# The shared expert's gate and up matmuls moved into the LN1 stage, a ring of eight weight matrices, and a routing mask by replacement

## What is computed

```python
mix = concat([y_pool, y_conv, y_mem]) @ w_out
x1 = layer_norm(alpha * x + mix, ln1_g, ln1_b)            # LN1
scores = sigmoid(x1 @ w_router)                            # 64 experts
_, idx = top_k(scores + router_bias, 8)
sel = take_along_axis(scores, idx)
gates = sel / sum(sel) * 2.5
# every expert e, for its tokens: 1024 -> 256 -> 1024
y_e = (silu(x1 @ w_gate[e]) * (x1 @ w_up[e])) @ w_down[e] * gate
shared = (silu(x1 @ w_gate_sh) * (x1 @ w_up_sh)) @ w_down_sh   # every token
x = layer_norm(alpha * x1 + routed + shared, ln2_g, ln2_b)     # LN2
```

## Time and profile before

| | us |
|---|---|
| median of 3 runs | 1502.26 (1501.83 to 1504.17) |
| profiled execution | 1498.6 |
| its span, first to last instruction | 1497.0 |
| PE busy in it | 1355.4 (91%) |
| DVE busy | 989.9 (66%) |
| ACT busy | 776.2 (52%) |
| POOL busy | 469.7 (31%) |
| mean granted TensorE clock | 0.942 of 2.4 GHz |

### The profile page before, as it was taken

The page is one execution under the profiler, slowest core; times in us unless marked ns, Lnnn a source line. Parts: engine busy times, 40 slices in busy tenths (PEclk is TensorE's granted clock), DMA queues, the critical chain, the costliest instruction groups (busy, mean ns, idle before and its releaser), DMA issues. The chain is left out here.

```text
span 1497.0 us, 25821 instructions
## 1 busy us (share of the span) xinstructions
PE 1355.4 (91%) x6447; PEld 1115.0 (74%) x6448; DVE 989.9 (66%) x1164; ACT 776.2 (52%) x1031; POOL 469.7 (31%) x433
## 2 busy tenths in 40 slices
PE   8968937799879999999999999999999999999965
PEld 7856626577767887888888788888888887788842
DVE  4599656367776377676577645557577577677718
ACT  4122155221133376776577646657677577677710
POOL 0000010136644224333343333333333434433321
PEclk9988967798879999999999999999999999999978
DMA  6121050222345489898889978888899899998745
GB/s 228 43 70 56 0 187 8 85 85 85 86 157 200 148 295 342 260 337 283 250 300 318 344 229 250 255 250 249 267 305 323 280 323 349 327 322 272 233 150 211
DMA packets 77249, 327.89 MB, mean 219 GB/s; under 512 B 22720, under 2 KB 22832, under 8 KB 51744
## 3 DMA queue, kind: packets, MB, share of 16 engines
q1 hardware_dynamic: 41360, 251.05, 44.9%
q0 software_dynamic: 34704, 72.23, 20.0%
q10 hardware_dynamic: 1152, 4.19, 0.7%
HBM read 294.65 MB, written 67.34 MB: 242 GB/s over the span
## 5 line engine op out<-in xcount | busy, mean ns | idle before, releaser
L1494 PE MATMUL ps<-wgu,xTe 128*128 (+1 forms) x2496 | 597.7, 395 | 14.1 <-ACT wgu L696 9.7
L1494 PEld LDWEIGHTS ps<-wgu,xTe 128*128 128x128 f32 x2496 | 463.5, 189 | 111.2 <-issue 18.5
L1512 PE MATMUL ps<-wdn,hT 128*128 (+1 forms) x1236 | 297.3, 389 | 0.0
L1197 DVE TENSOR_TENSOR wgu<-raw,wgu (+1 forms) x130 | 292.1, 2289 | 5.5 <-issue 3.1
L1512 PEld LDWEIGHTS ps<-wdn,hT 128*128 128x128 f32 x1236 | 232.0, 188 | 48.2
L696 ACT CAST wgu<-raw (+1 forms) x130 | 250.0, 1925 | 29.1 <-SPq L395 28.4
L1202 DVE TENSOR_TENSOR xTe<-ps,xTe 128x512 fp32r<-128x512 f32 x210 | 134.9, 684 | 140.6 <-ACT xTe L748 138.0
L1197 DVE TENSOR_TENSOR wdn<-raw,wdn (+1 forms) x65 | 149.0, 2293 | 53.6 <-ACT wdn L741 52.5
L753 ACT ACTIVATE ysb<-ps,idx 128x512 f32<-128x512 f32 x188 | 119.1, 685 | 118.7 <-PE ps L1512 118.7
L539 POOL DMA_INDIRECT xa_d<-ysb,idx x48 | 88.0, 1834 | 259.6 <-ACT ysb L753 208.6
L539 POOL DMA_INDIRECT xb_d<-ysb,idx x47 | 88.5, 1883 | 241.7 <-ACT ysb L753 224.7
(11 more groups left out here) (200 smaller groups left out, 1148.2 us busy)
## 6 DMA issues: line engine op xcount, KB each, us to landing
raw<-in_w_gate SPq DMA_DIRECT2D x64, 1024.0 KB
raw<-in_w_up SPq DMA_DIRECT2D x64, 1024.0 KB
raw<-in_w_down SPq DMA_DIRECT2D x64, 1024.0 KB
wraw<-in_w_in SPq DMA_DIRECT2D x10, 512.0 KB, 3.3
xin<-in_x SPq DMA_DIRECT2D x8, 512.0 KB, 7.0
wraw<-in_w_kv SPq DMA_DIRECT2D x8, 512.0 KB, 3.3
raw<-in_w_out SPq DMA_DIRECT2D x4, 1024.0 KB, 7.9
xres<-in_x SPq DMA_DIRECT2D x8, 512.0 KB
```

The costliest lines, as they stand in the source:

```text
L1197: V.tensor_tensor(dst, raw_, hi.bitcast(F), ALU.subtract).then_inc(done, 1)
L1494: last = mm(ps[:, 2 + s, :], xTe[:, s, st, d], wgu[:, w, mo, d].rearrange("p a n -> p (a n)"), start=(d == 0 and st == 0 and mo == 0), sto ...
L1512: last = mm(ps[:, 5 + h, :], hT[:, s, st, c], wdn[:, w, mo, c, h * 512:(h + 1) * 512].rearrange("p a n -> p (a n)"), start=(c == 0 and st ...
```

## The change

**PE's order in the LN1 stage.** A round now does both halves of the projection of tile t + 1, then the transposes of tile t, the rank sums of tile t-1, the gate and up matmuls of the shared expert for tile t-1 from its `x1T` (now two buffers), and the logits of tile t. The weights stand in `wsh`, the results in banks 1 and 4; ACT's silu and DVE's product `hxs` follow in the LN1 loops. The rows are not loaded and transposed a second time.

**The rest of the shared expert.** Seven tiles' hidden transposes and down matmuls follow the stage; the eighth tile's lie in the first routed step. ACT itself issues the stores of their results.

**Normalisation.** ACT's part goes; DVE subtracts the mean and multiplies by the gain, then multiplies by the reciprocal root and adds the offset.

**Routing.** The eight best scores are replaced by a large negative number, and the mask is where the array changed. Addresses come from the largest eight of mask x (list start + rank).

**Ring.** `raw` is a ring of eight matrices; matrix n of expert e has place (3e + n + 1) mod 8. SP requests the loads one matrix at a time, in the order in which the places come free. The loads of LN2's gain and offset are issued after the last split of weights, before it was after the item tables.

```diff
--- before.py
+++ after.py
-        xTe = at("xTe", 96, [128, 2, 2, ND, 128], R)
-        raw = at("raw", 112, [128, 2, 3, 2048])
+        xTe = at("xTe", 184, [128, 2, 2, ND, 128], R)
+        raw = at("raw", 96, [128, SLOTS, 2048])
...
-        x1T = at("x1T", 152, [128, 2, ND, 128], R)
+        wsh = at("wsh", 96, [128, 2, ND, 512], R)
+        wshr = at("wshr", 112, [128, ND, 512])
+        wdnr = at("wdnr", 72, [128, 2, D])
+        x1T = at("x1T", 144, [128, 2, 2, ND, 128], R)
+        hxs = at("hxs", 184, [128, NT - 1, XD])
...
+        def shared_bank(u):
+            return (1, 4)[u % 2] if u < NT - 1 else 3
+        def slot_of(e, n):
+            return (3 * e + n + 1) % SLOTS
...
-            for n, w in enumerate(("sh_gate", "sh_up", "sh_down")):
-                sp.dma_start(raw[:, 0, n], a[w]).then_inc(s_rwd[0] if n == 2 else s_rw[0], 16)
+            for n, w in enumerate(("sh_gate", "sh_up")):
+                sp.dma_start(wshr[:, :, n * XD:(n + 1) * XD],
+                             a[w].rearrange("p (c n) -> p c n", c=ND)).then_inc(s_shw, 16)
...
-            def load_expert(e, s, nth):
...
-                sp.wait_ge(s_glo, 2 * e - 2)
-                load("w_gate", 0, s_rw[s])
-                load("w_up", 1, s_rw[s])
-                sp.wait_ge(s_rw[1 - s], 32 * nth)
-                sp.sem_inc(s_ready, 1)
-                sp.wait_ge(s_dlo, e - 1)
-                load("w_down", 2, s_rwd[s])
-                sp.wait_ge(s_rwd[1 - s], 16 * nth)
-                sp.sem_inc(s_dready, 1)
+            def load_expert(e0, rounds):
+                e = e0 + SLOTS * rounds
+                if e0 == 2:
+                    sp.wait_ge(s_lg, NT)
+                    sp.wait_ge(s_gu, NT)
+                elif e0 >= 4:
+                    sp.wait_ge(s_glo, 2 * e - 4)
+                load(e, 0, slot_of(e0, 0))
+                for n in range(2):
+                    landed(e0 - 1, n, rounds)
+                sp.sem_inc(s_ready, 1)
+                if e0 >= 4:
+                    sp.wait_ge(s_dlo, e - 2)
+                load(e, 1, slot_of(e0, 1))
+                landed(e0 - 1, 2, rounds)
+                sp.sem_inc(s_dready, 1)
+                if e0 >= 3:
+                    sp.wait_ge(s_glo, 2 * e - 3)
+                load(e, 2, slot_of(e0, 2))
...
@@ scalar @@
+            def shared_silu(u):
+                act.wait_ge(s_gu, u + 1)
+                if 2 <= u < NT - 1:
+                    act.wait_ge(s_h, u - 1)
+                dst = hss[:, u % 2] if u < NT - 1 else hs[:, 1]
+                nc.scalar.activation(dst, ps[:, shared_bank(u), 0:XD], ACT.Silu).then_inc(s_silu, 1)
...
-                    nc.scalar.activation(xres[:, t % 2], xres[:, t % 2], ACT.Identity,
-                                         bias=rs[:, 1:2], scale=rs[:, 0:1]).then_inc(s_hat, 1)
...
+            for t in range(NT):
+                if t + 2 < NT:
+                    mix_hi(t + 2)
+                if t == NT - 1:
+                    shared_silu(t - 1)
+                x1_hi(t)
+                if 1 <= t < NT - 1:
+                    shared_silu(t - 1)
+                scores_of(t)
...
+            for u in range(NT - 2):
+                hidden_hi(u + 1)
+                if u == 2:
+                    act.wait_ge(s_ready, 2)
+                    gate_up_hi(1, 0)
+                    gate_up_hi(1, 1)
+                if u >= 2:
+                    act.wait_ge(s_ysh[u % 2], 16 * (u // 2))
+                act.wait_ge(s_dn, u + 1)
+                y_out(u % 2, 1.0 / ALPHA)
+                put_shared(u)
...
@@ vector, route @@
-                step(V.max_index(idxu[:], top8[:], sb_[:]))
-                settle()
-                step(V.tensor_copy(idxf[:, u], idxu[:]))
-                settle()
-                step(V.tensor_tensor(oh[:], iotaE[:].unsqueeze(1).to_broadcast([128, K, E]),
-                                     idxf[:, u].unsqueeze(2).to_broadcast([128, K, E]), ALU.is_equal))
-                settle()
-                step(V.tensor_reduce(maskf[:], oh[:].rearrange("p k e -> p e k"), AX.X, ALU.add))
-                settle()
-                step(V.tensor_copy(maskb[:], maskf[:]))
+                step(V.match_replace(rest[:], top8[:], sb_[:], -1e30))
+                settle()
+                step(V.tensor_tensor(maskb[:], rest[:], sb_[:], ALU.not_equal))
+                step(V.tensor_tensor(maskf[:], rest[:], sb_[:], ALU.not_equal))
...
@@ vector, LN1 loop @@
-                step(V.tensor_tensor(xres[:, r], xres[:, r], g1[:], ALU.mult))
-                settle()
-                V.tensor_tensor(xres[:, r], xres[:, r], b1[:], ALU.add).then_inc(s_x1, 1)
+                if t >= 1:
+                    x1_lo(t - 1)
+                step(V.scalar_tensor_tensor(x, x, mv[:, 0, 0:1], g1[:], ALU.subtract, ALU.mult))
+                v.wait_ge(s_pw, 2 + t)
+                settle()
+                V.scalar_tensor_tensor(x, x, rs[:, 0:1], b1[:], ALU.mult, ALU.add).then_inc(s_x1, 1)
+                if t >= 2:
+                    rank(t - 2)
+                    shared_hidden(t - 2)
+                if t >= 1:
+                    route(t - 1)
...
+            rank(NT - 1)
+            hidden_lo(0)
+            item_tables()
+            hidden_lo(1)
+            hidden_lo(2)
+            item_tables_out()
+            hidden_lo(3)
+            gate_up_lo(1, 0)
+            hidden_lo(4)
+            gate_up_lo(1, 1)
+            hidden_lo(5)
+            hidden_lo(6)
...
@@ tensor @@
+            for t in range(NT):
+                if t + 1 < NT:
+                    for h in range(2):
+                        project(t + 1, h)
+                else:
+                    shared_gate_up(t - 1)
+                x1_transposed(t)
+                if t >= 1:
+                    ranks(t - 1)
+                if 1 <= t < NT - 1:
+                    shared_gate_up(t - 1)
+                logits(t)
+            shared_gate_up(NT - 1)
...
+            for u in range(NT - 1):
+                if u + 1 < NT - 1:
+                    hidden_transposed(u + 1)
+                down(u, u % 2, 0)
+                if u == 1:
+                    item_tables()
```

More of the change, by code:

```diff
@@ L48 @@
 RING = 8
+SLOTS = 8
 ALWAYS = (NT + E) // RING
@@ new lines, in _ @@
+            pe.wait_ge(s_oe, 2 * HEADS)
+            for h in range(2):
+                project(0, h)
+            pe.wait_ge(s_wrl, 1)
+            for t in range(NT):
+                if t + 1 < NT:
+                    for h in range(2):
+                        project(t + 1, h)
[7 more added lines that the diff above has]
+                logits(t)
```

502 lines of the change are left out of this document (239 added, 263 removed).

## The result

The changed kernel takes **1479.95 us** (median of 4 runs, 1477.48 to 1480.28) against 1502.05 for the kernel before in the same session: ratio 0.9849, 95% interval 0.9824 to 0.9875. It is 22 us faster; the forecast was 44. The profiled execution took 1479.69 us, its span is 1478.1 us.

What follows compares the result with a forecast made beforehand. PE bounds it: the LN1 stage in small pieces at clock 0.85, the routed loop with 24.3 us of stalls. 1498.6 - 25.5 (earlier routed start) - 19 (ring) = 1454.1 profiled, 1458 us for the median; range 1444 to 1486.

Steps and rivals of the forecast that it cites:

- two cases in the 1470s: Rivals: DMA engines limit the routed loop, 1474 us, chance 0.14; the new LN1 stage throttles, 1473 us, chance 0.12.
- two bounds of the stage: Gain at the first routed start: 30 us with no half clock and first down 2 us late; 8 at worst.
- signs named: Next profile: routed start 492 to 500 us, rounds 20 to 21, downs some 4 apart, weight waits under 8.
- The LN1 rounds: Six equal PE rounds in the LN1 stage, together 20.2 us each, 121.3 in all, without the former 2.39 us waits.
- I charge it once: Half clock after PE waits in the LN1 stage or the downs: 4.9 us, added once, moving the start to 496.5.
- The row of downs: Seven shared downs after the LN1 stage: 19.1 us of matmuls plus exposed latencies, 35.2 us, ending at 487.3.
- the last scatters, the tables and the first gather: Beside the row of downs: estimated done some 8 us before the downs end, counted as nothing.
- gathers come late behind weights: Rival: loop gathers delayed by one more weight matrix in flight, 2.0 us late on half the items, 1554 us; chance 0.06.
- The ring: Eight matrices in the routed loop: two more lie ready per run of single-item experts, absorbing 19 of 24.3 us of stalls.
- Routing by replacement: DVE in the LN1 rounds: some 1.5 us a tile less, hidden under PE, taken at nothing.
- The new stage throttles: Rival: PE's waits at tile 0, tile 7 and in the downs each bring half clock, 1473 us; chance 0.12.
- The engines limit the loop: Rival: full DMA engines, not the ring, limit the routed loop; gain 3 instead of 19 us, 1474 us; chance 0.14.

Runs made afterwards that it cites:

- e5: Changed kernel with tile 7's transposes ahead of tile 6's shared gate and up, and hidden low halves ahead of last rank and item tables: 1472.14 us.
- e8: e1 plus only e5's new order of the last round; the last rank stays ahead of the first hidden half: 1461.17 us.
- e1: Changed kernel with SP's loads of expert 2 held until the stores of the first four shared tiles have landed: 1464.4 us.
- e2: Changed kernel with four buffers of their own for shared results 2 to 5, so ScalarE waits for no store: 1477.55 us.
- e3: Changed kernel, eight ring places kept, but SP waits before loads as in the kernel before, never more than six matrices ahead: 1494.2 us.
- e6: Changed kernel with e1's hold of the weights and both of e5's new orders together: 1464.5 us.
- e7: e6 with own buffers for shared results 2 to 5 and the weights held until GpSimd's first gather is issued: 1464.26 us.
- e9: e6 with a scatter address buffer for each tile instead of two in turn: 1464.12 us.
- e10: e7 with a scatter address buffer for each tile: 1460.35 us.
- e11: e8 with a scatter address buffer for each tile: 1462.31 us.
- e12: e10 with the weights of expert 2 held until the first gathered rows have landed, not until their gather is issued: 1455.51 us.
- e4: Changed kernel with two unused one-hot operations and a reduction added back to each tile's routing on DVE: 1478.05 us.

## Why the prediction was right and where it failed

**Direction and range: right, the range in part by luck.** The shared matmuls and the ring both gain, and 1479.95 lies in 1444 to 1486. Its upper part was there for two cases in the 1470s; the half clock was one of them, the wait for the store, 8.3 us, was in none. The likeliest time, 1458, was 22 us too low. For the profiled execution the sum was 1454.1 and the time is 1479.69: 25.6 us to account for. They are 21.3 in the start of the first routed gate and up (496.5 forecast, 517.8 measured), 2.4 in the loop (2.3 of them the half clock in the first routed gate and up), 1.9 in the tail. Of the signs named, the rounds and ACT's waits for weights (3.4 us) came as forecast, the start and the distance of the downs did not. The two bounds of the stage were added up wrongly: from the terms named they are 33 and 7, not 30 and 8, and the measured 4.2 lies below either.

**The LN1 rounds: right.** Six rounds were put at 20.2 us each. Five take 20.1 without a gap; the first takes 22.8, because its projection still runs at half clock for a part (13.89 us instead of 11.16). What fell is "I charge it once". Half clock came at the logits of tile 0 and at those of tile 7 (rows of the profile after), about 5 us each: the last shared gate and up end at 460.4, 8.3 us past the 452.1 in which neither was charged. 4.9 of these 8.3 had been charged. e5 and e8 took the second away: the order alone gives 6.2 us ahead of the downs. The Trainium skill, "TensorE: Matmul & The Clock Gate", section on HAM oscillation, has waits between bursts paid again by the clock; the traces agree for these two places.

**The row of downs: the step that failed.** It was put at 35.2 us with 4.3 behind it, and took 57.4 (460.44 to 517.83), 17.9 more. The largest part is at the fourth down. I had put 3.7 us there, for two conversions on ACT; they took 3.7 (479.79 to 483.49), and then ACT waited 8.4 more for a landed store, so that the fourth down started 12.0 us after PE was ready: 8.3 over. Then 4.0 are half clock in two downs (4.51 and 5.46 us instead of 2.97 and 3.01), 3.1 the first down (7.8 us after the last gate and up instead of 4.7, of which 2.7 are the late silu; in e1, e2 and e3 it is 5.1), 2.1 the opening of the first routed item (6.4 us instead of 4.3), and 0.4 the rest. The working looked at latencies of engines alone, and had a row that said otherwise: in the earlier trace rows a load of 0.5 MB behind three weight matrices was waited for until 12.2 us after its issue. I used it for the gathers of the loop and not for the stores. It asked of no queue what its transfers wait for, though two of them lie on the path: the stores of `ysb`, which has two buffers and now takes a result every 4 us instead of every 9.3, and "the last scatters, the tables and the first gather run beside the downs; I estimate them done some 8 us before the downs end, and count nothing". The gather was issued at 499.35 us, 12.2 us before the downs ended (511.6), and did not hold PE there. Where the store no longer does, this chain can set the start: in e2, e6, e7, e9, e10, e11 and e12 PE waits for gathered rows (in e1, e3 and e8 it does not). The hold alone (e1) makes the row 43.9 us, 4.4 over the forecast. e12 starts 2.7 us ahead of my 496.5, but with the new order of the last round in it.

**The cause is what SP does, shown by e1, and by e3 with fewer weights.** I counted SP's weight requests in the loop and not at the place where the change releases them. Before, SP requested expert 2 from 446.98 to 450.37 us, and then no weights until

```profile
489.29 0.33 SPq L390 DMA_DIRECT2D raw<-in_w_gate  x1
```

Now the request of expert 2 waits for the last shared gate and up (`s_gu` in the diff; the ring lies over `wsh`), so it goes out just ahead of the downs, and there is room for four matrices at once. The rival "gathers come late behind weights" was this mechanism; I placed it in the loop, where no row of after shows it, and gave it 0.06. Beside it I cited the Trainium skill, "DMA: Bandwidth & Descriptors", section on queues and rings: an engine takes turns between queue rows by packet. Here that did not protect a small transfer: 18.0 us for 0.5 MB behind weights, 2.7 (e1) to 4.9 (e6) at most without them. The measurement decides; which part of the way is slow there (169 GB/s at a share of 1.04) stays open.

**The ring: right.** 19 was forecast, 16.6 came in the loop; e3 shows that it is the ring.

**Routing by replacement: right**, priced at nothing (e4).

**The other rivals.** "The new stage throttles" gave 1473 for three more half clocks, 14.7 us. Half clock came at all three places it names, 4.9, 5.0 and 4.0 us, of which 4.9 had been charged: this rival, with a chance of 0.12, holds 9.0 of the 21.3 us at the start, and the wait for the store 8.3. That the two are separate causes e1 shows, which takes the store's wait and leaves the half clock at tile 7 (logits 5.15 us). "The engines limit the loop" is refuted by 3.4 us of waits at the same share of 0.87.

## What to carry to other kernels

When work is taken out from between short steps, ask each queue what it will start at the moment when the cover goes: a prefetch that is released at the head of a row of small stores, scatters and gathers delays them all, and one wait on SP was worth 10 to 15 us (e1), against 22 for the whole change. Follow the chain to its last transfer: a hold that ends one transfer too early gave e6, e7 and e9 nothing on e1 for the waits they removed, and moved to the landing of that transfer it gave 4.8 us (e12 against e10, medians of two sessions). A buffer only moves such a wait on to the next chain; price both chains before choosing between more buffers and a later prefetch. A wait of PE that one group of matmuls can cover may be worth more than its length: 1.94 us at tile 7 were worth 6.2 in e5, because the groups behind it then also ran at full clock.

## What the runs showed of the hardware

In the changed kernel a wait of 2.38 us and one of 1.94 us between dense matmuls were each followed by half clock for about 10 us of matmuls, a loss of 5 us; in e2 the same 1.94 us cost 3.4. A wait of 2.1 to 2.2 us between two downs was followed by half clock in e7 and e9 (4.6 us instead of 3.0) and not in e6 and e8, so the length of the wait alone does not tell. DMA engines at a busy share of 1.04 moved 169 GB/s in one stretch and 376 at 1.02 in another: the share tells that engines are occupied, not that they move much. A scatter of 128 pairs keeps GpSimd for 1.28 us, and GpSimd waited 5.3 us (e10) to 9.8 (e11) for the last ones to land, with no weights requested meanwhile, against 16.5 in the changed kernel. A gather of 128 rows of 4 KB took 5.1 and 5.6 us from its issue to the landing of its rows (e5, e12), and 11.0 beside four new weight requests (e10).
